# Moving the weight slabs of a two-block inference kernel from 64 B to 128 B modulo 512 B in SBUF

## What is computed

```python
def reference(x, ...):
    x = first_block(x, ...)      # RMS norm + state-space mixer, RMS norm + latent attention, final norm
    return second_block(x, ...)  # sparse attention + convolution branch, feed-forward, gated embedding, norm

# nearly all of the arithmetic is in projections like these
proj = u @ in_w                                    # state-space and latent attention inputs
h = h + y.astype(u.dtype) @ out_w                  # outputs of both mixers
z = u @ w_in[i]                                    # second block
v = rmsnorm(h, g_ffn[i]) @ w_up[i]                 # 1024 x 5632
h = h + (jax.nn.gelu(v_gate) * v_val) @ w_down[i]  # 2816 x 1024
```

## Time and profile before

| | us |
|---|---|
| median of 3 runs | 857.76 |
| lowest, highest | 855.22, 858.75 |
| profiled execution, its own time | 856.84 |
| its span, first to last instruction | 855.1 |
| PE busy (share of the span) | 835.9 (98%) |
| PE weight loads busy | 804.2 (94%) |
| POOL busy | 623.2 (73%) |
| DVE, ACT busy | 527.4 (62%), 485.5 (57%) |

### The profile page before, as it was taken

How to read it: one execution, slowest core, us unless ns; L and a number is a source line. 1 busy time by engine, 2 the same in 40 slices (tenths; PEclk the granted TensorE clock), 3 DMA queues, 4 the chain that set the end, 5 groups by cost and what they waited for, 6 DMA issues and landing times.

```text
span 855.1 us, 18202 instructions
## 1 busy us (share of the span) xinstructions
PE 835.9 (98%) x7017; PEld 804.2 (94%) x7017; DVE 527.4 (62%) x1543; ACT 485.5 (57%) x925; POOL 623.2 (73%) x282
## 2 busy tenths in 40 slices
PE   8999999999999999999999999999999999999995
PEld 8999988889998899999999989988999999999995
DVE  5997658873244535445458998875666676641164
ACT  6754466664546456563846457875644544554362
POOL 3899855655997455554889899454968888889681
PEclk9999999999999999999999999999999999999998
DMA  8667633332775343434566667433646566667511
GB/s 324 201 215 218 188 121 100 100 99 72 217 221 161 120 137 112 145 101 124 154 217 189 184 203 227 136 88 117 199 142 209 181 189 182 189 190 224 179 50 50
DMA packets 38678, 138.46 MB, mean 162 GB/s; under 512 B 4416, under 2 KB 4544, under 8 KB 38592
## 3 DMA queue, kind: packets, MB, share of 16 engines
q1 hardware_dynamic: 38592, 137.30, 52.4%
HBM read 136.23 MB, written 1.05 MB: 161 GB/s over the span
## 4 chain that ended last, share of the span: by engine, by line
PE 77%; DVE 5%; ACT 2%; issue 1%; POOL 1%; DVEq 0%; ACTq 0%
PE ps L640 21%; PE ps L642 20%; PE ps L641 20%; PE ps L861 1%; DVE ps L1730 1%; POOL wl L583 1%; PE ps L647 1%; PE ps L767 1%; ACT wh L1132 1%; PE ps L649 1%; PE ps L648 1%; PE ps L667 1%; DVE cx L1994 1%; PE ps L885 1%; PE ps L994 1%
## 5 line engine op out<-in xcount | busy, mean ns | idle before, releaser
L583 POOL TENSOR_TENSOR wl<-raw,wh 128x1024 fp32r<-128x1024 f32 x254 | 606.0, 2412 | 192.0 <-ACT wh L1132 191.6
L640 PE MATMUL ps<-uh,wh 128*128 128x256 f32 (+1 forms) x1248 | 353.1, 283 | 1.8 <-POOL wl L583 0.8
L642 PE MATMUL ps<-uh,wl 128*128 128x256 f32 (+1 forms) x1248 | 348.9, 280 | 0.0
L641 PE MATMUL ps<-ul,wh 128*128 128x256 f32 (+1 forms) x1248 | 348.8, 279 | 0.0
L1132 ACT ACTIVATE wh<-raw 128x1024 fp32r<-128x1024 f32 (+1 forms) x255 | 262.8, 1052 | 83.9 <-PE ps L642 76.4
L640 PEld LDWEIGHTS ps<-uh,wh 128*128 128x128 f32 (+1 forms) x1248 | 234.5, 188 | 3.6 <-issue 1.6
L641 PEld LDWEIGHTS ps<-ul,wh 128*128 128x128 f32 (+1 forms) x1248 | 236.4, 189 | 0.0
L642 PEld LDWEIGHTS ps<-uh,wl 128*128 128x128 f32 (+1 forms) x1248 | 233.8, 187 | 0.1
L1823 DVE TENSOR_TENSOR h<-ps,h 128x256 f32<-128x256 f32 x32 | 13.6, 424 | 101.7 <-PE ps L642 101.6
L641 PE MATMUL ps<-ffl,wh 128*128 128x256 f32 x176 | 49.5, 281 | 0.0
L640 PE MATMUL ps<-ffh,wh 128*128 128x256 f32 x176 | 49.5, 281 | 0.0
(11 more groups left out here) (363 smaller groups left out, 1680.2 us busy)
## 6 DMA issues: line engine op xcount, KB each, us to landing
raw<-slabs SPq DMA_DIRECT2D x255, 512.0 KB, 4.1
h<-x_fm SPq DMA_DIRECT2D x4, 256.0 KB, 4.7
out_fm<-outb SPq DMA_DIRECT2D x4, 256.0 KB, 2.2
cst<-shape_consts SPq DMA_DIRECT2D x1, 768.0 KB, 9.4
vec<-vectors SPq DMA_DIRECT2D x1, 299.5 KB, 9.2
pin<-p_fm SPq DMA_DIRECT2D x1, 256.0 KB, 4.8
raw<-slabs SPq DMA_DIRECT2D x1, 128.0 KB, 2.7
vec<-vectors SPq DMA_DIRECT2D x1, 4.0 KB, 2.4
```

The lines of the kernel that those rows point to most:

```text
L583: nc.gpsimd.tensor_tensor(wl[:, s % PART_RING, :], raw[:, s % RAW_RING, :], wh[:, s % PART_RING, :].bitcast(f32), ALU.subtract).then_inc(s ...
L640: nc.tensor.matmul(res, w_h, a_h, start=first, stop=False)
L641: nc.tensor.matmul(res, w_h, a_l, start=False, stop=False)
L642: ins = nc.tensor.matmul(res, w_l, a_h, start=False, stop=last)
```

## The change

One constant is changed. It is used in the one call of `start_at` above, so `raw`, `wh` and `wl` each start 64 B higher, at 128 modulo 512. The gap ahead of them is 448 B in place of 384, the gap behind 384 in place of 448, and every other tile keeps its address.

```diff
@@ -58,7 +58,7 @@
 FIRST_COLS = 8
 WARM_UP = 20
 PIECE = 512
-STATIONARY_AT = 64
+STATIONARY_AT = 128
 
 
 def weight_jobs():
```

## The result

The changed kernel is slower. Its median is 868.38 us (4 runs, 868.20 to 868.73), that of the kernel before 858.08 us over the 4 runs beside it (855.22 to 858.75): ratio 1.018, interval 1.013 to 1.024. The profiled execution took 868.20 us around a span of 866.3 us, so 1.9 us lie outside and the span grew by 11.2 us. The forecast had been 857 us with a range up to 867 us, so the time fell outside, on the side of rival C but beyond its price.

The account below looks back on a forecast made before the run. TensorE's matmul count times spacing was taken to bound the kernel; with slab feeding at zero and the same two spacings in about the same shares, the base of 857 us stayed 857.0, with 8 in 10 from 842 to 867.

Parts of the forecast that it names:

- rival C: Short-spacing stretches and attention runs turn long, 4.5 ns a step: slower, 866 us, with a longer spacing 875 and more; chance 0.28.
- What bounds the kernel: TensorE, busy 835.9 of 855.1 us: the time is the number of matmuls times their start-to-start spacing.
- Feeding the slabs at zero: DMA, ACT pass (1052 ns) and POOL pass (2412 ns) of each slab cost nothing more; bound for POOL +0.5 us a slab.
- The two spacings read at 64 B: Projection matmuls on TensorE start 113.2 ns apart in the `mh` stage and 117.9 ns in the `ffh` stage.
- a lock: How TensorE's stationary load and moving stream settle into one spacing, said to hold until something interrupts TensorE.
- The swapped roles: `vsw`, `hk`, `hv` projections: weights are the moving tile, stationary block 64 B below the stream; both spacings were read there.
- the three short stretches: 398 to 438, 440 to 482 and 595 to 628 us, 1,016 records at short spacing; all must turn long for "slower".
- The third spacing: A longer spacing on TensorE, possible but without a row; one further step on the long stretches would add 17 us.
- Rival A: All projection stages keep the same two spacings in about the same shares: 857 us, within 4; chance 0.38.
- Rival B: Stationary block farther from the stream's head, long spacing goes: 850 us for feed-forward and down projections, 840 for all; chance 0.34.
- The port rule: Weight loads and the running matmul have read ports of their own on TensorE, so the shift could not matter.
- The base: The unchanged kernel's time, taken as 857 us from three runs of 855.22 to 858.75 us with median 857.76.

Follow-up runs that it names:

- the sweeps: TensorE alone, no other engine working, stationary tiles at many offsets modulo 512 B and several entries: 113.3 to 120.0 ns a step; no time of the whole kernel.
- equal-distance twin: Against the kernel before, `raw`, `wh`, `wl` at 128 B and streamed tiles at 64 B, so the distance stays 64 B: 855.13 us, ratio 1.004.
- 24 entries: TensorE alone, stationary tiles at 64, 128, 192 and 56 B, each entered in 24 ways from a standstill: at 128 B 118.5 to 120.0 ns a step.
- the first run: Only `raw` moved to 128 B against the kernel before, `wh` and `wl` left at 64 B: 864.23 us, ratio 1.016.
- the second run: The same kernel with only `raw` at 128 B, run once more against the kernel before: 867.85 us, ratio 1.016.

## Why the prediction was wrong

*What bounds the kernel.* Right. TensorE's steps set the time; nothing else moved. The steps grew by 15.0 us for a growth of 11.3, the rest being taken up in the standstills for the most part, which the sum had not allowed for.

*Feeding the slabs at zero.* Right for this change: 2409 and 1052 ns, and with `wh` and `wl` alone moved the time is the same. The reason given, that `raw`, `wh` and `wl` keep their places against each other, turned out to matter more than I knew: with `raw` moved alone the kernel loses 1.6%, though not by longer passes but by VectorE instructions of 13 us, TensorE's wait behind them and the half clock that follows.

*The two spacings read at 64 B.* Right, and so is that a lock is caught at the entry and then held.

*"So a distance other than 64 B has the same two spacings, and a change of distance does not give a new one."* This is the step that failed. The swapped roles put the stationary block 64 B below the stream, and I took this one other distance for any distance. It is the mirror image: 64 B under is 192 modulo 256, and 192 B is the one other offset in the sweeps at which 113.3 and 117.8 are both caught (3 and 21 of 24). The whole kernels bear this out: in the changed one the swapped roles stand 128 B apart like all others, and none of their 136 steps is short; with the constant at 192 they stand at 64 modulo 256, and 89 of 135 are in runs at 113 to 115 ns. The rows had a faint hint that I smoothed over: the earlier trace rows shows 280 ns for the long spacing of the swapped roles, where 64 B has 281. `mh` with the constant at 192 B, at 117.8 ns a step, is not at 281 either:

```profile
L640 PE MATMUL ps<-mh,wh x64: 279/279/279, 608.8 to 631.1; 128*128 128x256 f32 x64
```

*Rival C and its price.* The sign was C's, and it decides as I put it, with the three short stretches gone. But its price was bounded by all steps at 117.8, 9.2 us; the spacings at 128 B are 118.7 and 120.0, so the 2,050 short steps lost 5.4 ns and more each and the 3,700 long ones lost 0.9 ns too: 2,053 x 5.4 + 3,698 x 0.9 = 14.4 us, and 0.4 more for the 298 steps around `mh` at 120.0. The third spacing that I called possible without a row, and put beyond the range, is what came. Rival A had the most weight, on the failed step alone. Rival B's thought, farther from the head of the stream is better, has no support: 128 B is worse than 64, 224 better than 192, and 0 and 160 worst.

*The port rule.* The sentence of the Trainium skill ("TensorE: Matmul & The Clock Gate", Step-by-step: what each phase is for), that loading weights does not steal read bandwidth from the running matmul, would have kept the time. The sweep disagrees: with all other engines still, the distance of the two addresses moves the step between 113.3 and 120.0 ns. The measurement decides.

*The range.* 842 to 867 left out 868.4. The base was too firm as well: before spreads over 846 to 859 us in all its runs here, and my reading is that the lock of the long stretch is drawn anew from execution to execution (117.8 in its profile, 113.3 in that of its equal-distance twin; 1,555 steps at 4.4 ns are 6.9 us of the 13), while the changed kernel stays within 0.6 us: its two spacings are only 1.3 ns apart, and 22 of the 24 entries at 128 B came out below 119.

*Still open.* By what mechanism the distance of the two addresses sets the step, and why in units of 32 B, is not shown; that the two reads get in each other's way is my picture of it, and I only measured that the step follows the distance. Nor is it shown what in the entry picks the lock, what holds up VectorE for 13 us when `raw` lies 64 B above `wh` (that it is GpSimd's passes is argued from their timing alone), and what of the spread of the kernel before comes from other stretches than the longest.

## What to carry to other kernels

If TensorE runs float32 three-pass products back to back, with a load of 128 columns and a stream of 256 for each step, put stationary and streamed operands at a fixed distance and sweep it once in a kernel of a hundred lines that runs nothing else; here the result carried over to the nanosecond and spans 6%. Where a trace shows two spacings for the same instruction, look at how the stretch was entered before looking at anything else: a cheap standstill may buy the better one, and the trace has to show that it did. And a distance seen in the trace is evidence for that distance only, a mirrored one least of all for others.

## What the runs showed of the hardware that I had not expected

The step of a stationary load of 128 columns with a stream of 256 (float32, fp32r) depends on the distance of the two addresses, with a period of 256 B and in steps of 32 B: 113.3 or 117.8 ns at 40 to 64 B, 117.3 or 118.7 at 72 to 96, 118.7 or 120.0 at 104 to 128, 120.0 at 136 to 160, 117.8 and rarely 113.3 at 168 to 192, 116.7 at 200 to 224, 120.0 at 232 to 256, 118.3 at 8 to 32.

Some distances have two stable spacings. Once caught, one held for 1,555 steps, 183 us. In the kernel with 24 entries one further matmul of a single column at the entry changed which was caught, and a fall and rise of the granted clock did so in two runs. At half clock the step was 213.3 ns whatever the distance.

A VectorE instruction on 32 x 256 elements took 12.9 us in one run and 12.7 in another, while GpSimd's passes followed one another without a gap. Below are the six passes of the first run: they ended at 57.8 us, and the VectorE instruction of 45.2 us ended 0.2 us behind them. In the second run it ended 0.2 us behind the last of seven.

```profile
43.80 14.03 POOL L584 TENSOR_TENSOR wl<-raw,wh 128x1024 fp32r<-128x1024 f32 x6
```
